# Order of the opening of a two-layer conv/HGRN2 inference step on one Trainium2 core: weight loads behind two more input rows, products split into interleaved terms

## What is computed

```
for i in range(2):                       # layer 0: gated short conv, layer 1: HGRN2
    h = rms_norm(x, norm_pre[i])         # 1024 prompt rows and 8*4 sample rows, d_model 1024
    proj = h @ w_in[i]                   # 1024 x 4096: v, bg, cg, z in layer 0
    o = mixer(proj) * silu(z)            # layer 0: bg * conv3(cg * v) * silu(z)
    x = x + rms_norm(o @ w_out[i], norm_post[i])
```

## Time and profile before

| | us |
|---|---|
| median of 3 runs | 1033.07 |
| the profiled execution's own time | 1033.07 |
| its span on the core | 1031.2 |
| PE busy | 1021.6 (99%) |
| DVE busy | 713.4 (69%) |
| ACT busy | 419.0 (41%) |
| groups of the opening end, first block product begins (weight load) | 67.15 |

### The profile page before, as it was taken

One profiled execution on the slowest core, in us unless ns is written; L12 is line 12 of the kernel. 1 busy time (PEld: TensorE's weight loads), 2 busy tenths in 40 slices (PEclk: granted clock), 3 DMA queues, 4 the chain that ended last, 5 costly groups with the idle time before them and its releaser, 6 DMA issues.

```text
span 1031.2 us, 20565 instructions
## 1 busy us (share of the span) xinstructions
PE 1021.6 (99%) x7915; PEld 970.6 (94%) x7915; DVE 713.4 (69%) x1282; ACT 419.0 (41%) x844; POOL 18.2 (2%) x45
## 2 busy tenths in 40 slices
PE   9999999999999999999999999999999999999998
PEld 8999999999999978889999999999999999997886
DVE  6899677677776926762858778585877858586355
ACT  7444333333333624443345443433534343383222
POOL 1000000000000000000000000000000000000000
PEclk9999999999999999999999999999999999999999
DMA  8002121112112253322213221221322122153064
GB/s 254 22 22 82 42 82 41 41 51 71 41 41 61 102 170 115 123 82 56 56 54 85 63 54 50 69 73 46 82 61 62 42 70 75 54 179 108 26 242 168
DMA packets 130369, 82.96 MB, mean 80 GB/s; under 512 B 37782, under 2 KB 121703, under 8 KB 130327
## 3 DMA queue, kind: packets, MB, share of 16 engines
q1 hardware_dynamic: 112438, 73.39, 23.9%
q10 hardware_dynamic: 17888, 8.98, 3.0%
HBM read 64.72 MB, written 13.44 MB: 76 GB/s over the span
## 4 chain that ended last, share of the span: by engine, by line
PE 85%; DVE 8%; issue 3%; ACT 3%; ACTq 0%; DVEq 0%; POOL 0%; POOLq 0%
PE bank L749 28%; PE bank L692 26%; PE bank L837 14%; PE bank L717 4%; PE bank L1092 3%; PE bank L931 2%; PE bank L1048 1%; PE bank L1041 1%; PE bank L1050 1%; DVE arena L2316 1%; ACT L1465 1%; DVE wsplit L1735 1%; PE bank L819 1%; PE bank L1035 1%; PE bank L854 1%
## 5 line engine op out<-in xcount | busy, mean ns | idle before, releaser
L692 PE MATMUL bank<-reg_a,wsplit 128*128 128x352 f32 x2304 | 382.2, 325 | 2.8 <-DVE wsplit L1735 2.8
L692 PEld LDWEIGHTS bank<-reg_a,wsplit 128*128 128x128 f32 x2304 | 368.5, 188 | 6.0 <-issue 4.5
L749 PE MATMUL bank<-reg_a,wsplit 128*128 128x264 f32 x1344 | 165.7, 284 | 0.0
L749 PEld LDWEIGHTS bank<-reg_a,wsplit 128*128 128x128 f32 x1344 | 164.1, 188 | 0.2 <-DVE arena L1922 0.2
L749 PE MATMUL bank<-reg_b,w_ring 128*128 128x264 f32 x1008 | 124.6, 284 | 0.0
L749 PEld LDWEIGHTS bank<-reg_b,w_ring 128*128 128x128 f32 x1008 | 123.3, 188 | 0.0
L837 PE MATMUL bank<-reg_b,reg_a 128*128 128x512 f32 x288 | 69.3, 396 | 0.0
L837 PEld LDWEIGHTS bank<-reg_b,reg_a 128*128 128x128 f32 x288 | 53.7, 188 | 12.6 <-issue 0.4
L1950 DVE TENSOR_TENSOR arena<-arena,bank 128x264 f32<-128x264 f32 x84 | 34.8, 428 | 34.1 <-PE bank L749 33.0
L1313 ACT ACTIVATE arena<-bank 128x264 f32<-128x264 f32 x84 | 32.2, 390 | 55.5 <-PE bank L749 50.8
L1291 ACT ACTIVATE w_ring<-wraw 128x512 fp32r<-128x512 f32 x42 | 26.1, 631 | 69.0 <-PE bank L749 69.0
(11 more groups left out here) (297 smaller groups left out, 1485.7 us busy)
## 6 DMA issues: line engine op xcount, KB each, us to landing
wraw<-in_w_in SPq DMA_DIRECT2D x64, 512.0 KB, 4.1
first_x<-in_x_prompt SPq DMA_DIRECT2D x8, 512.0 KB, 6.9
wraw<-in_w_out SPq DMA_DIRECT2D x8, 512.0 KB, 3.7
w_out_raw<-in_w_out SPq DMA_DIRECT2D x8, 512.0 KB, 5.1
arena<-in_w_out SPq DMA_DIRECT2D x8, 512.0 KB, 5.2
arena<-in_x_prompt SPq DMA_DIRECT2D x8, 512.0 KB, 3.4
x_scratch<-arena SPq DMA_DIRECT2D x8, 512.0 KB, 2.6
arena<-arena SPq DMA_DIRECT2D x128, 32.0 KB, 1.9
```

Source lines behind the costliest of these rows:

```text
L692: mm = nc.tensor.matmul(bank[b][:, 0:CH], w[wi][:, k, :], rhs[hi], start=(k == 0 and i == 0), stop=(k == KT - 1 and i == 2))
L749: mm = nc.tensor.matmul(bank[banks[q]][:, 0:QT], w[wi][:, k, :], B_OP[name][hi][:, k, q * QT:(q + 1) * QT], start=(start and k == 0 and i ...
```

## The change

The loads of weight tiles 0 and 1 are issued behind input rows 5 and 6 instead of 3 and 4. TensorE turns rows 0 to 4 before the first product, and the products of tiles 0 and 1 are written as three functions of eight products each (`first_high`, `first_weight_low`, `first_token_low`) that are interleaved between two tiles and around the turns of rows 5 to 8. Tiles 2 and 3 keep whole groups. ACT takes the norm of row 4 ahead of the first splits and splits the first quarter's halves around `first_hi(0)`. DVE scales turned rows and writes low token parts by halves, in another order.

```
--- before.py
+++ after.py
@@ -416,9 +416,9 @@
                 load_input(i)
                 if i == 1:
                     load_vector(norm_pre, PRE, 2, pre_in)
-                if i == 3:
+                if i == 5:
                     load_w(0, wsrc(w_in[0], 0), 0, 0, False)
-                if i == 4:
+                if i == 6:
                     load_w(1, wsrc(w_in[0], 2 * D), 1, 0, False)
             for src, row, n in ((norm_post, POST, 2), (conv_w[0], CW, 3), (lb_logits, LBL, 1)):
                 load_vector(src, row, n, vec_in)
@@ -697,26 +697,43 @@
                 return [wsplit[:, i, 0], wsplit[:, i, 1]]
 
 
-            def first_group(g):
-
-                t, q = (g % 2, g // 2) if g < 2 * NQ else (g // NQ, g % NQ)
-                b = J0_BANK[g % 4]
-                pe.wait_ge(bank_free[g % 4], emptied(g // 4))
+            def first_term(t, q, wi, hi, first, last):
+
+                g = 2 * q + t if t < 2 else t * NQ + q
+                cols = slice(q % 2 * QT, (q % 2 + 1) * QT)
+                for k in range(KT):
+                    if t < 2 and k % KH == 0:
+                        if hi:
+                            pe.wait_ge(S_LO.sem, S_LO.at(q, f"lo{k // KH}"))
+                        else:
+                            pe.wait_ge(S_AT.sem, S_AT.at(q, f"hi{k // KH}"))
+                    src = B_OP[(("m1", "m4"), ("m2", "m3"))[k // KH][q // 2]]
+                    mm = nc.tensor.matmul(bank[J0_BANK[g % 4]][:, 0:QT], slot(t % 2)[wi][:, k, :], src[hi][:, k % KH, cols],
+                                          start=(first and k == 0), stop=(last and k == KT - 1), skip_group_check=t < 2)
+                return mm
+
+            def first_high(t, q):
+
+                pe.wait_ge(bank_free[(2 * q + t) % 4], emptied(q // 2))
                 pe.wait_ge(w_hi, t + 1)
-                w = slot(t % 2)
-                cols = slice(q % 2 * QT, (q % 2 + 1) * QT)
-                for i, (wi, hi) in enumerate(((0, 0), (1, 0), (0, 1))):
-                    for k in range(KT):
-                        if i == 0 and k % KH == 0:
-                            pe.wait_ge(S_AT.sem, S_AT.at(q, f"hi{k // KH}"))
-                        elif i == 1 and k == 0:
-                            pe.wait_ge(w_lo, t + 1)
-                        elif i == 2 and k % KH == 0:
-                            pe.wait_ge(S_LO.sem, S_LO.at(q, f"lo{k // KH}"))
-                        src = B_OP[(("m1", "m4"), ("m2", "m3"))[k // KH][q // 2]]
-                        mm = nc.tensor.matmul(bank[b][:, 0:QT], w[wi][:, k, :], src[hi][:, k % KH, cols],
-                                              start=(k == 0 and i == 0), stop=(k == KT - 1 and i == 2))
-                mm.then_inc(proj_done, 1)
+                first_term(t, q, 0, 0, True, False)
+
+            def first_weight_low(t, q):
+
+                pe.wait_ge(w_lo, t + 1)
+                first_term(t, q, 1, 0, False, False)
+
+            def first_token_low(t, q):
+                first_term(t, q, 0, 1, False, True).then_inc(proj_done, 1)
+
+            def first_group(t, q):
+
+                pe.wait_ge(bank_free[q], emptied(t))
+                pe.wait_ge(w_hi, t + 1)
+                first_term(t, q, 0, 0, True, False)
+                pe.wait_ge(w_lo, t + 1)
+                first_term(t, q, 1, 0, False, False)
+                first_term(t, q, 0, 1, False, True).then_inc(proj_done, 1)
 
             def turn_weights():
 
@@ -724,19 +741,43 @@
                 nc.tensor.transpose(bank[7][:, 0:2 * KT], st_vec[0:2 * KT, :], ident[0:2 * KT, 0:2 * KT]).then_inc(K_PE, 1)
 
             keep_busy(23)
-            START = {3: (0,), 4: (1,), 6: (2, 3), 7: (4,)}
-            for i in range(TT):
+            turn_input(0)
+            turn_weights()
+            for i in range(1, 5):
                 turn_input(i)
-                if i == 0:
-                    turn_weights()
-                for g in START.get(i, ()):
-                    if g == 3:
-                        pe.wait_ge(K_DVE, 1)
-                    first_group(g)
-            for g in range(5, 4 * NQ):
-                if g == 6:
-                    turn_constants()
-                first_group(g)
+            first_high(0, 0)
+            first_weight_low(0, 0)
+            first_high(1, 0)
+            first_token_low(0, 0)
+            first_weight_low(1, 0)
+            first_token_low(1, 0)
+            turn_input(5)
+            first_high(0, 1)
+            pe.wait_ge(K_DVE, 1)
+            first_high(1, 1)
+            first_weight_low(0, 1)
+            first_weight_low(1, 1)
+            turn_input(6)
+            first_token_low(0, 1)
+            turn_input(7)
+            first_token_low(1, 1)
+            turn_input(8)
+            first_high(0, 2)
+            first_high(1, 2)
+            first_weight_low(0, 2)
+            first_weight_low(1, 2)
+            first_token_low(0, 2)
+            turn_constants()
+            first_high(0, 3)
+            first_token_low(1, 2)
+            first_high(1, 3)
+            first_weight_low(0, 3)
+            first_weight_low(1, 3)
+            first_token_low(0, 3)
+            first_token_low(1, 3)
+            for t in (2, 3):
+                for q in range(NQ):
+                    first_group(t, q)
 
             def block_product(p, name, banks, start, guards):
 
@@ -1224,9 +1265,9 @@
                     act.wait_ge(proj_done, 2 * NQ - 1 + t % 2)
                 A(wsplit[:, t % 2, 0], wraw[:, t % 2], ACT.Copy).then_inc(w_hi, 1)
 
-            def token_hi(q):
-
-                for kk in range(2):
+            def token_hi(q, halves=(0, 1)):
+
+                for kk in halves:
                     act.wait_ge(S_DT.sem, S_DT.at((2, 4, 6, 8)[q], ("ta", "tb")[kk]))
                     A(B_OP[(("m1", "m4"), ("m2", "m3"))[kk][q // 2]][0][:, :, q % 2 * QT:(q % 2 + 1) * QT],
                       h_raw[:, kk * KH:(kk + 1) * KH, q * QT:(q + 1) * QT], ACT.Copy).then_inc(S_AT.now(f"hi{kk}"), 1)
@@ -1245,16 +1286,16 @@
 
             act.wait_ge(eps_set, 1)
             A(small[:, 47:48], eps[:, :], ACT.Sqrt)
-            for i in range(4):
+            for i in range(5):
                 normalise(i)
+            token_hi(0, (0,))
             first_hi(0)
-            token_hi(0)
-            normalise(4)
+            token_hi(0, (1,))
             first_hi(1)
             for i in (5, 6):
                 normalise(i)
+            token_hi(1)
             first_v(0)
-            token_hi(1)
             normalise(7)
             normalise(8)
             token_hi(2)
@@ -1759,10 +1800,10 @@
-            def token_lo(q):
+            def token_lo(q, halves=(0, 1)):
...
-                for kk in range(2):
+                for kk in halves:
@@ -1805,29 +1846,39 @@
             V.tensor_copy(cst[:, 0:2 * KT], bank[7][:, 0:2 * KT]).then_inc(K_DVE, 1)
             dve.wait_ge(K_DVE, 1)
             scale_turned(0)
+            scale_turned(1, (0,))
             normalise(2)
-            scale_turned(1)
+            scale_turned(1, (1,))
             normalise(3)
             scale_turned(2)
+            normalise(4)
+            token_lo(0, (0,))
+            scale_turned(3, (0,))
             first_lo(0)
-            token_lo(0)
-            normalise(4)
+            scale_turned(3, (1,))
+            token_lo(0, (1,))
             first_lo(1)
-            scale_turned(3)
+            scale_turned(4, (0,))
             normalise(5)
...
```

More of the change, by code:

```diff
@@ L1807, in _ @@
             scale_turned(0)
+            scale_turned(1, (0,))
             normalise(2)
-            scale_turned(1)
+            scale_turned(1, (1,))
             normalise(3)
             scale_turned(2)
+            normalise(4)
+            token_lo(0, (0,))
+            scale_turned(3, (0,))
             first_lo(0)
-            token_lo(0)
-            normalise(4)
+            scale_turned(3, (1,))
+            token_lo(0, (1,))
             first_lo(1)
-            scale_turned(3)
+            scale_turned(4, (0,))
             normalise(5)
-            scale_turned(4)
+            scale_turned(4, (1,))
             normalise(6)
-            token_lo(1)
-            scale_turned(5)
-            scale_turned(6)
+            scale_turned(5, (0,))
+            token_lo(1, (0,))
+            scale_turned(5, (1,))
+            token_lo(1, (1,))
             normalise(7)
+            scale_turned(6, (0,))
             normalise(8)
+            scale_turned(6, (1,))
             first_u(0)
-            token_lo(2)
-            scale_turned(7)
-            scale_turned(8)
+            scale_turned(7, (0,))
+            token_lo(2, (0,))
+            scale_turned(7, (1,))
+            scale_turned(8, (0,))
+            token_lo(2, (1,))
+            scale_turned(8, (1,))
+            token_lo(3)
             first_u(1)
-            token_lo(3)
             constants()
```

## The result

The changed kernel took 1035.76 us, the kernel before 1033.29 us in the same rounds (medians of 11 runs each): a ratio of 1.0025, 95% interval 1.0016 to 1.0033, or +2.47 us. The forecast was +2.5 us. One of the twelve executions of the run `searched` further down took 2604 us, the others at most 1035.56; its median of 1033.98 hardly depends on it.

What follows compares the result with a forecast made beforehand. TensorE was 99% busy, with VectorE's chain from the end of tile 0, quarter 3 as second bound. An opening 0.58 us later plus a group end 1.95 us later gave +2.5 us, 1035.5 us, range 1033.7 to 1036.7.

Steps and rivals of the forecast that it cites:

- fixed length: VectorE's chain from the start of `first_lo(2)` to the end of the `first_gate` pair: 26.2 us, whatever its start.
- Steps 1 and 2: Opening: row 2 turned from about 11.11 us, 0.60 later scaled identity; row 4 turned from 14.8, a wait of 0.1.
- Step 3: Opening: the first term needs no wait, although tile 0's weights land later, at about 13.75 us.
- Step 4: Opening: TensorE's second term waits 1.06 us, until 17.71, for VectorE's `first_lo(0)`.
- Step 5: Opening after `first_lo(0)`: TensorE runs dense, two groups end at 22.58 us, TensorE is 0.58 us later than before.
- Step 6: Last groups before tile 2: 8 products, not 24, stand behind tile 0, quarter 3, so it ends 1.95 us later.
- The parts that TensorE pays: Waits: 0.8 us for tile 2's high part, 0.3 its low part, 0.5 tile 3's bank, the rest at m1's second quarter.
- The low part in time: Rival, opening: `first_lo(0)` ends before 16.6 us and the opening's waits vanish; +0.7 us, 1033.8 us, chance 0.13.
- The chain that does not bind: Rival: TensorE pays only the 0.8 us wait for tile 2's high part beside 0.58; 1034.5 us, chance 0.07.
- The slip: Rival, opening until 22 us: a late half on VectorE costs another 1 us; 1036.6 us, chance 0.11.
- The clock: Rival: 27 products behind the 1.06 us wait run at half pace, 3.3 us; 1038.9 us, chance 0.02.
- Absorbed: Rival: a later TensorE wait for something not moved takes up the delay; 1033.1 us, chance 0.07.

Runs made afterwards that it cites:

- searched: Kernel before with the opening's order laid out anew and the gates moved ahead of token low part l6: 1033.98 us against 1033.45.
- loads_back: Changed kernel with tiles 0 and 1 loaded behind input rows 3 and 4 again: 1036.03 us against 1033.21 for the kernel before.
- row2_tail: Changed kernel with row 2's scaled identity behind two halves and tile 0's last group finished before tile 1's: 1033.52 us against 1033.27 before.
- tail_whole: Changed kernel with tile 0's last group finished before tile 1's begins: 1033.84 us against 1033.33 for the kernel before.
- before_tail8: Kernel before with groups 6 and 7 interleaved so that 8 products, not 24, stand behind tile 0's quarter 3: 1035.21 us against 1033.33.
- before_tail16: Kernel before with groups 6 and 7 mixed so that 16 products stand behind tile 0's quarter 3: 1034.26 us against 1033.33.
- row2_early: Changed kernel with row 2's scaled identity made behind two scaled halves, not three: 1035.24 us against 1033.33 for the kernel before.
- row2_tail_gate: Changed kernel with row 2's identity behind two halves, tile 0's last group finished first and gates ahead of l6: 1034.62 us against 1033.45 before.
- before_loads: Kernel before with only the loads of tiles 0 and 1 moved behind rows 5 and 6: 1034.66 us against 1033.21.

## Why the prediction was right

- *What bounds.* That TensorE at 99% stands level with VectorE at the end of the opening was read from one wait of 0.21 us. The two doses show it: eight and sixteen products less behind the last group of tile 0 cost 0.12 us each. The chain's "fixed length" is fixed only to a quarter of a microsecond: from the start of `first_lo(2)` to the last pair of gates it took 25.45 us before, 25.38 in the change and 25.21 in loads_back, and VectorE's idle time for the load inside it was 0.50 us before, 0.58 in the change and 0.32 in row2_tail.
- *Steps 1 and 2.* Row 2 from 11.21, row 4 from 14.91 (11.11 and 14.8). The 0.1 us is that of this execution's first rows, turned by 0.1 later than before (8.56 against 8.46 for row 1). Undoing step 1 gave back 0.56 by the medians and 0.60 by the trace.
- *Step 3.* The first term had its weights and tokens. Undoing the load order showed what I had not said: it was row 4's earlier landing, not the weights' later one, that mattered. That SyncE "waits for room on its queue anyway" was not read from the rows shown: in the kernel before one issue of an input row takes 4.80 us where most take 0.43, in the changed kernel one takes 3.59, and what SyncE waits for there no run shows.
- *Step 4.* The wait was 1.03 us (1.06) and was released by `first_lo(0)`.
- *Step 5.* TensorE is 0.58 us later at the end of the opening: tail_whole, where only that is left, gave +0.51, and its first block product begins 0.58 us later behind row 1 than before (67.82 - 8.55 against 67.15 - 8.46).
- *Step 6.* 1.95 us by count, 1.96 by tail_whole (1.99 by its trace) and 1.88 by before_tail8.
- *The parts that TensorE pays.* 0.8, 0.3, 0.5 and the rest were forecast; idle 0.79, 0.16, 0.45 and 0.50 were recorded. The 0.3 was somewhat too much.
- *Left to the end.* 2.56 us at 81.64 us; median +2.47.
- *Bank changes at no cost.* 56 loads in a row take 6.89 us in the change, where the bank changes with every term of eight (from 37.66 us), and 6.89 us in tail_whole, where it changes half as often (from 37.64 us). row2_tail still interleaves terms and has nothing left by its trace.
- *The rivals.* The low part in time: it came 1.03 us late. The chain that does not bind: before_tail16 decides against it. The slip: no. The clock: the 40 products behind the wait ran at 0.12 us; the 27 products of that rival's price had no row behind them. Absorbed: no, m5 begins 2.56 us later and the median is 2.47 up.
- *The rule on waits.* The Trainium skill, page "TensorE: Matmul & The Clock Gate", section "A second HAM failure mode: psum-queue depth-cycling", speaks of frequent short idle times between groups of products, and for the few waits of 0.2 to 1.0 us in the changed kernel's trace, at a granted clock of nine tenths or more in every slice, it is not borne out. A kernel that waits as often as that section means was not run.

The forecast was right in its parts, not by luck: each term of the sum came out within 0.15 us. What I did not see in advance is how short the slack is just behind the opening: I named none for m5, and the gates' move ran into it. The forecast did not need it, since the change moves both sides alike.

## What to carry to other kernels

When two accumulation groups are interleaved, look at who waits for the one that used to end early: its end moves towards the end of both, and if its reader starts a chain that is level with the bounding engine, every product of the move is paid for, as here with eight and with sixteen. A busy share of 99% does not mean that the engine leads; one short wait on another queue at the end of a stretch can mean that the two bounds lie close together. Before an instruction is moved ahead in a queue, ask what it waits for itself, since all that is behind it waits too. Differences of half a microsecond that the medians cannot tell were plain in the traces once times were counted from a fixed place behind the uneven start.

## What the hardware showed unexpectedly

The turning of row 0, 16 passes of one form, took 1.87 us in the kernel before, 1.93 in the changed kernel and 2.45 in row2_early, where nothing ahead of it or in it differs on TensorE. It took 2.34 in row2_tail and 2.28 in row2_tail_gate, 2.00 in before_loads, and 1.86 in the other eight runs. That all three runs with row 2's earlier identity are slow here can be chance: that identity is made behind row 0. Row 1, the same form, took 1.86 us wherever it stands by itself in the view. The windows of row2_early's profile count fewer weight loads for each us up to 8 us, six and then eight, where the kernel before has nine and eleven from 6 us on, with a granted clock of 1.00 in every one. The columns are the stretch, its length, busy time and count of PE, PEld, DVE, ACT and POOL, the granted clock, the DMA share and GB/s. Of row2_early:

```profile
6.00:7.00 1.00, 1.00 (x7) 1.00 (x6) 0.23 (x1) 1.00 (x2) 0.86 (x6) 1.00 1.02 410
7.00:8.00 1.00, 1.00 (x8) 1.00 (x8) 0.45 (x2) 0.77 (x2) 0.09 (x2) 1.00 1.02 414
```

and of the kernel before:

```profile
6.00:7.00 1.00, 1.00 (x10) 1.00 (x9) 0.24 (x1) 0.97 (x3) 0.86 (x6) 1.00 0.76 299
7.00:8.00 1.00, 1.00 (x12) 1.00 (x11) 0.45 (x2) 0.16 (x1) 0.10 (x2) 1.00 1.02 385
```

So TensorE's first products run slower for a time that differs between executions of the same start, up to about 0.6 us here, and the granted clock of these rows does not show it. What ends it was not tried. It is one reason why the whole time of a single profile is no measure for half a microsecond here; a median of some eleven executions, or times counted from row 1 on, serve better.
